# A decoder layer with a PEER expert sub-layer: 32 prompt tokens leave the dense expert pass for the gathered-row path (192 dense, 96 gathered)

## What is computed

```python
def _peer(h, wq, keys, u_tab, v_tab):          # per block of tokens tb
    q = (tb @ wq).reshape(TOK_BLOCK, PEER_HEADS, 2, PEER_DK)
    s = jnp.einsum('thpd,hpkd->thpk', q, keys)
    sv, si = lax.top_k(s, PEER_TOPK)
    ...                                         # top 16 of 16 x 16 sums, per head: fv, i1, i2
    eid = (i1 * PEER_NKEYS + i2).reshape(TOK_BLOCK, PEER_HEADS * PEER_TOPK)
    g = jax.nn.softmax(fv, axis=-1).reshape(TOK_BLOCK, PEER_HEADS * PEER_TOPK)
    hid = jax.nn.gelu(jnp.einsum('td,ted->te', tb, u_tab[eid]), approximate=False)
    return jnp.einsum('te,ted->td', (g * hid), v_tab[eid])
```

## Time and profile before

| | us |
|---|---|
| median of 3 runs | 2441.48 (2439.57 to 2441.72) |
| the profiled execution, its own time | 2438.12 |
| span of its profile | 2436.3 |
| gate rounds (line 1394 first to last) | 937.2 to 1026 |
| groups 0 and 1 | 1043.9 to 1172.0 |
| body(2), body(3) | 1172.0 to 1348.6 |
| body(4) to body(11) | 1348.6 to 2106.0 |
| body(12) | 2106.0 to 2193.5 |
| body(13), body(14) | 2193.5 to 2358.4 |
| V of the last group | 2358.4 to 2412.9 |

### The profile page before, as it was taken

The page is one execution under the profiler, slowest core; times in us unless marked ns, Lnnn a source line. Parts: engine busy times, 40 slices in busy tenths (PEclk is TensorE's granted clock), DMA queues, the critical chain, the costliest instruction groups (busy, mean ns, idle before and its releaser), DMA issues.

```text
span 2436.3 us, 38402 instructions
## 1 busy us (share of the span) xinstructions
PE 2257.6 (93%) x14756; PEld 1965.1 (81%) x14756; DVE 1645.2 (68%) x2907; ACT 925.3 (38%) x1034; POOL 355.9 (15%) x316
## 2 busy tenths in 40 slices
PE   7699999767979988999999999999999999999986
PEld 2298888436859988988999888888888888889985
DVE  1259777324345697866888777777877777766775
ACT  0332332342243314634444343343443443444432
POOL 1043000200000004510011212222212222010000
PEclk9899999778989999999999999999999999999999
DMA  9867776766634534576777999888989889877652
GB/s 382 349 234 288 286 277 226 279 242 225 236 127 145 163 131 153 216 250 234 266 273 282 344 345 324 327 338 323 345 307 345 334 319 341 290 275 266 209 176 91
DMA packets 152112, 643.36 MB, mean 264 GB/s; under 512 B 16721, under 2 KB 17105, under 8 KB 133649
## 3 DMA queue, kind: packets, MB, share of 16 engines
q1 hardware_dynamic: 122112, 444.65, 51.8%
q0 software_dynamic: 28400, 187.90, 19.9%
q10 hardware_dynamic: 1440, 8.56, 0.8%
HBM read 618.05 MB, written 22.99 MB: 263 GB/s over the span
## 4 chain that ended last, share of the span: by engine, by line
PE 83%; DVE 7%; DMA 6%; ACT 3%; issue 1%; POOL 0%; SPq 0%; DVEq 0%; ACTq 0%
PE vb L1429 17%; PE zb L1412 15%; PE vb L1431 7%; PE zb L1414 7%; PE zb L481 6%; PE zb L483 6%; PE zb L482 6%; DMA ada_first<-in_w_ada 3%; PE zb L1374 3%; PE vb L1452 3%; PE vb L1441 2%; PE vb L1394 2%; PE vb L1102 2%; DMA cache<-in_cv 1%; PE vb L1428 1%; DVE lo L465 1%
## 5 line engine op out<-in xcount | busy, mean ns | idle before, releaser
L456 ACT ACTIVATE hi<-raw 128x1024 fp32r<-128x1024 f32 x624 | 659.5, 1059 | 1046.9 <-PE vb L1429 374.6
L465 DVE TENSOR_TENSOR lo<-raw,hi 128x1024 fp32r<-128x1024 f32 x624 | 765.3, 1229 | 359.4 <-ACT hi L456 354.8
L1412 PE MATMUL zb<-act_hl,hi 128*128 128x448 f32 x1792 | 575.6, 376 | 3.0 <-DVE lo L465 3.0
L1429 PE MATMUL vb<-w_rest,hi 128*128 128x448 f32 x1536 | 521.2, 378 | 0.0
L1414 PE MATMUL zb<-act_hl,lo 128*128 128x224 f32 x1680 | 444.7, 265 | 0.0
L481 PE MATMUL zb<-act_hl,hi 128*128 128x288 f32 x1152 | 347.2, 301 | 37.2 <-DVE act_hl L1561 37.2
L1412 PEld LDWEIGHTS zb<-act_hl,hi 128*128 128x128 f32 x1792 | 334.5, 188 | 52.3 <-issue 24.3
L1431 PE MATMUL vb<-w_rest,lo 128*128 128x224 f32 x1280 | 342.9, 268 | 0.0
L482 PE MATMUL zb<-act_hl,hi 128*128 128x288 f32 x1152 | 341.9, 297 | 0.0
L483 PE MATMUL zb<-act_hl,lo 128*128 128x288 f32 x1152 | 341.3, 296 | 0.0
L1414 PEld LDWEIGHTS zb<-act_hl,lo 128*128 128x128 f32 x1680 | 321.0, 191 | 5.0
(11 more groups left out here) (266 smaller groups left out, 2438.1 us busy)
## 6 DMA issues: line engine op xcount, KB each, us to landing
raw<-in_v SPq DMA_DIRECT2D x256, 512.0 KB, 5.3
raw<-in_u SPq DMA_DIRECT2D x224, 512.0 KB, 5.5
raw<-in_w_in SPq DMA_DIRECT2D x80, 512.0 KB, 9.4
ada_first<-in_w_ada SPq DMA_DIRECT2D x64, 512.0 KB, 8.7
ada_mid<-in_w_ada SPq DMA_DIRECT2D x64, 512.0 KB, 5.3
ada_in<-in_w_ada SPq DMA_DIRECT2D x32, 512.0 KB, 9.0
raw<-in_w_out SPq DMA_DIRECT2D x32, 512.0 KB, 4.2
ada_last<-in_w_ada SPq DMA_DIRECT2D x32, 512.0 KB, 6.9
```

Source lines behind the costliest of these rows:

```text
L456: act.activation(hi[s][:, :], raw[s][:, :], ACT.Copy).then_inc(hi_ready, 1)
L465: dve.tensor_tensor(lo[s][:, :], raw[s][:, :], hi[s][:, :].bitcast(F32), ALU.subtract) \
L1412: last = pe.matmul(zb[:, bank, 0:2 * ND], w_h, act_hl[:, k, :, 0:ND], start=(k == 0), stop=(k == KC - 1))
L1429: last = pe.matmul(vb[:, bank, 0:2 * ND], v_h, w[:, e % 2, :, :], start=(e == 0), stop=(e == GI - 1))
```

## The change

ND goes from 224 to 192, so NGT is 96: 64 prompt tokens and the 32 samples. The gathered path begins in group 1's V part (unit -24) and its tokens end in body(14), the last but one group. Chunks now come every 12/13 of a unit to unit 329, in body(12); tokens every 3.9 units from unit 14 to unit 396, with 6 more units between each 32. The rows of the 64 prompt tokens fill the 128 partitions of `h_rows` (high part and remainder), so the samples' rows have a second set, `h_rows_s`, for which there are further turns, copies and subtractions while the queries are projected. The buffers are laid out anew for the smaller ND. `hid_4` becomes a ring of 64 columns. The sums of the values are now turned three times instead of two, and `residual_gathered`, which stood between body(13) and body(14) on DVE, is called from inside body(14). All loops over the dense tokens shrink: a pair has 576 columns instead of 672, and there are 24 gate rounds instead of 28. The core of the diff:

```diff
-ND = 224
+ND = 192
...
-ROWS = 2 * NGT
+NR = 64
+ROWS = 2 * NR
 def chunk_unit(c):
-    return 5 * c // 4
+    return 12 * c // 13 - 24
 def token_unit(t):
-    return (58 if t < TS else 64) + 19 * t // 4
+    return 14 + 39 * t // 10 + 6 * (t // TS)
...
-    h_rows = [at(f"h_rows{b}", [ROWS, 2, 512], F32R, (x_at + 14336, peer + 68096)[b]) for b in range(2)]
-    pick = at("pick", [ROWS, NGT], F32R, peer + 96768)
+    h_rows = at("h_rows", [ROWS, 3, 512], F32R, x_at + 12288)
+    h_rows3 = at("h_rows3", [ROWS, 512], F32R, peer + 68096)
+    h_rows_s = at("h_rows_s", [P, 2, 512], F32R, peer + 70144)
+    pick = at("pick", [ROWS, NR], F32R, peer + 96768)
+    pick_s = at("pick_s", [P, TS], F32R, peer + 97024)
...
-            for g in range(2, NG - 2):
-                pool.wait_ge(w_ready, PP * g + PP)
-                load_gates(g + 2)
+            for g in range(1, NG - 1):
+                if 2 <= g < NG - 2:
+                    pool.wait_ge(w_ready, PP * g + PP)
+                    load_gates(g + 2)
...
-                    for b2 in range(2):
-                        act.activation(h_rows[b2][:, :, :], vb[:, 2 * b2:2 * b2 + 2, :], ACT.Copy).then_inc(hs_copied, 1)
-                    for r in (0, NGT):
-                        last = act.activation(pick[r:r + NGT, :], ident[r:r + NGT, r:r + NGT], ACT.Copy)
+                    act.activation(h_rows[:, :, :], vb[:, 0:3, :], ACT.Copy).then_inc(hs_copied, 1)
+                    act.activation(h_rows3[:, :], vb[:, 3, :], ACT.Copy).then_inc(hs_copied, 1)
+                    for r in range(0, P, NR):
+                        act.activation(pick[r:r + NR, :], ident[r:r + NR, r:r + NR], ACT.Copy)
+                    for r in range(0, P, TS):
+                        last = act.activation(pick_s[r:r + TS, :], ident[r:r + TS, r:r + TS], ACT.Copy)
                     last.then_inc(hs_copied, 1)
+                if j in (3, 4):
+                    act.wait_ge(hs_turned, j - 1)
+                    act.activation(h_rows_s[:, j - 3, :], vb[:, 2, :], ACT.Copy).then_inc(hs_copied, 1)
...
-                for r in (0, NGT):
-                    last = pe.matmul(vb[r:r + NGT, k // 4, P * (k % 4):P * (k % 4) + P], hF[:, k, ND:T], ident,
+                for r in (0, NR):
+                    last = pe.matmul(vb[r:r + NR, k // 4, P * (k % 4):P * (k % 4) + P], hF[:, k, ND:SEQ], ident,
                                      start=True, stop=True)
             last.then_inc(hs_turned, 1)
+            def turn_samples(part):
+                pe.wait_ge(hs_split, 2 + 2 * part)
+                for k in range(4):
+                    for r in range(4):
+                        last = pe.matmul(vb[TS * r:TS * r + TS, 2, P * k:P * k + P],
+                                         hF[:, 8 * (r // 2) + 4 * part + k, SEQ:T], ident, start=True, stop=True)
+                last.then_inc(hs_turned, 1)
...
-                    pe.wait_ge(hs_copied, 3)
+                    pe.wait_ge(hs_split, 6)
                 else:
                     pe.wait_ge(dots_done, c)
                 t, j = c // 4, c % 4
-                pe.matmul(vb[:, 3, :], pick[:, t:t + 1].to_broadcast([ROWS, P]), h_rows[j // 2][:, j % 2, :],
-                          start=True, stop=True).then_inc(spread, 1)
+                if t < NR:
+                    row = h_rows[:, j, :] if j < 3 else h_rows3[:, :]
+                    one = pick[:, t:t + 1].to_broadcast([ROWS, P])
+                else:
+                    half = slice(NR * (j // 2), NR * (j // 2) + NR)
+                    row = h_rows_s[half, j % 2, :]
+                    one = pick_s[half, t - NR:t - NR + 1].to_broadcast([NR, P])
+                pe.matmul(vb[:, 3, :], one, row, start=True, stop=True).then_inc(spread, 1)
...
+                beside(c - 24)
+            u_quad(Q_PEER + 10, 2, 2, -8)
+            u_quad(Q_PEER + 11, 3, 3, -4)
...
+                if c >= 64 and c % 32 == 0:
+                    dve.wait_ge(hid_kept, c // 32 - 1)
...
+                if n == token_unit(NGT - 1) + 14:
+                    residual_gathered()
...
-                u_quad(Q_PEER + 8 + pp, 2, pp, 0, 16)
-            for g in range(2, NG - 2):
+                u_quad(Q_PEER + 8 + pp, 2, pp, 0, 16, 4 * pp - 16)
+            for g in range(2, NG - 1):
```

139 lines of the change are left out of this document (71 added, 68 removed).

## The result

The changed kernel takes 2506.8 us (median of 4 runs, 2499.8 to 2515.4) against 2440.5 of the kernel before on the same chip: a ratio of 1.027 with an interval of 1.025 to 1.030. The prediction was 2352 us, a gain. The measured time is 155 us above it, and the change has the other sign.

What follows compares the result with a forecast made beforehand. PE's columns were taken to bound the main loop. Stage terms sum to -89.8 us, from the profiled 2438.1 to 2348.3, and 3.4 more for the median gives 2352 us, range 2322 to 2402.

Steps and rivals of the forecast that it cites:

- PE's price of a pair: Dense products on PE: a pair falls from 0.315 to 0.270 us, giving back 173 us over 3840 pairs.
- Rival E's half form: Dense pairs on PE: only the narrow product stays unshrunk, pair 0.279 us, +35 us, 2387 us in all; chance 2%.
- A spread chunk costs 0.30: PE in the bodies: each spread chunk takes 0.30 us, four of them in a gathered token's 2.2 us.
- A full body has 34.7 chunks: Gathered bodies: 69.1 us of pairs, 10.4 of chunks and 7.8 of tokens make 87.3 us on PE.
- Rival C: Bodies: DVE becomes the bound through hand-offs, bodies of 93 us, +31, 2383 us in all; chance 10%.
- Rivals A and B: Gathered bodies: DMA queues bound at 371 GB/s (2398 us, 13%), or memory at 357 GB/s (2431 us, 3%).
- Rival D: Gathered bodies: u rows land too late, whole gain gone at 13.5 us mean landing, 2536 us at 15; chance 3%.
- Gate rounds, -12.3: Gate rounds before group 0: 28 become 24 (-7.1) and the 96 products beside them shrink by a seventh (-5.2).
- Group 0, -6: Group 0, 54.0 us: 160 narrower pairs would give -7.2, taken as -6 because a raw load shows.
- Group 1, -0.8: Group 1, 74.1 us: 224 narrower pairs -10.1, 31 added chunks +9.3; DVE tight, +3 at worst.
- Body(13), (14), -13.2: The two bodies before the last group: 164.9 to 151.7 us, with 11 tokens and an added turn of sums.
- The last group, -5: Last group, 54.5 us: 128 narrower pairs would give -5.8, but part is a chain through ACT and DVE.

Runs made afterwards that it cites:

- the third kernel: The changed kernel with the samples' spreads over all 128 partitions and one chunk per unit: 2414.0 us, 0.990 of the kernel before.
- the first experiment: The changed kernel with only the samples' spreads contracted over all 128 partitions, zero-filled, instead of 64: 2461.9 us, 1.010 of the kernel before.
- experiment 9: The kernel before with most dense pairs cut to 384 and 192 columns, sums of 32 dense tokens left incomplete: 2363.6 us, 0.970 of before.
- experiment 6: The kernel before with its 256 spreads on 128, 96, 64 or 32 partitions, changed every 26 spreads, some rows left out: 2502.6 us, single run.
- experiment 5: The changed kernel with full-height sample spreads, one chunk per unit, and v gathers fetching 16 rows, not 128, from the third token on: 2404.8 us, 0.986 of before.
- experiment 8: The kernel before with chunks coming two at a time every 2.5 units, so 128 units have two: 2640.8 us, single run.

## Why the prediction was wrong, point by point

The miss is 154.8 us. It closes: 62 from 2352 to the third kernel, 48 for the doubles (first to third experiment), 45 for the half-height spreads. In the other order the last two are 59 and 34; why they overlap by 11 us isn't shown.

- **PE's price of a pair** is the first step that failed. "Scaling the pair gives 0.315 x 576/672 = 0.270", measured 0.287. The check on 288-column products compared two products of 288 with one of 384 and one of 192. The experiments show both numbers to be right, 0.266 at (288, 288) and 0.284 to 0.287 at (384, 192): the total was the same, the split was not. Over 3840 pairs 0.017 would be 65 us, and the third kernel is 62 from the forecast. That the two agree so well is partly chance, as experiment 9 shows the price to hold only where PE has no gaps: from body(2) to body(12) the pairs are 48 us of the miss, while groups 0 and 1 and the end missed by more than their pairs. The other end of the price, 0.275 from pure column time, was no bound either.
- **Rival E's half form**, in which the narrow product gives nothing back, was the right mechanism. It had 2 in 100 and a pair of 0.279, still 0.008 short. The prediction shows no working for 0.279. With the forecast's own price per column, 64 columns less make 0.315 - 64 x 0.315/672 = 0.285, and with pure column time 0.315 - 64/2400 = 0.288; these put the time at 2410 and 2421, above the stated range and on either side of the third kernel's 2414. The point given for the whole rival, no gain from 0.2935 on, came out well: at 0.287 it leaves 3840 x 0.0065 = 25 us, and the third kernel gained 26.
- **"A spread chunk costs 0.30"** is the second step that failed. It holds for prompt tokens (0.61 around a spread, of which the pair's own part is 0.29 to 0.31). For the 128 sample chunks it was 0.65. The diff has it in plain sight, `slice(NR * (j // 2), ...)`, and no row of before shows a product of this height among full ones. It should have been bounded as an unknown operation. The Trainium skill's rule on a change of tiling mode (TensorEngine Tiling (Array Packing), "Key Properties"), told under experiment 6, would have opened a rival.
- **"A full body has 34.7 chunks"**, with nothing said about two of them in one unit, is the third, a wait put at nothing. The forecast priced 12/13 of a unit as a rate. What counted is that a second spread waits in PE's order for the dot of the first, with the whole dense stream queued behind it. I listed DVE's slack and never asked which engine waits for it. Before had one chunk at most per unit. The 30 doubles cost 48 us, 1.6 each.
- **Rival C**, DVE the bound, is not it: DVE is busy 77 to 79 us a body, as forecast (77.3; its narrower operations, 28 of 0.620 us less a seventh, are 2.5 and not 2.7), and the third kernel has the same DVE work in 92.0 us. PE did wait on DVE, but for one bank.
- **Rivals A and B**, DMA: refuted as a bound of 94.6 and 98.3. The queues moved 377 GB/s in body(4) of the changed kernel, above A's 371. Of them only the 9 us of experiment 5 were seen. **The friction of 2.2 us a body** was 1.1 in the third kernel.
- **Rival D** had the right side and the wrong reason: rows landed in 8.9 us in the median, never above 11.6, below its 13.5.
- **Gate rounds, -12.3**: first to last product now 931.6 to 1005.7 where it was 937.2 to 1024.9, 13.6 less. Right. All stages up to group 0 gave 20.1 in the changed kernel and 13.8 in the third; forecast 15.2.
- **Group 0, -6**: -1.8. **Group 1, -0.8**: +5.0, and +4.1 in the third kernel, beyond the +3 given as the worst. Experiment 9, with no chunks there, gained 2.1 where its pairs should have given 6, so these groups don't follow PE's columns. Part of it is the clock: one less the granted clock, times the length, comes to 9 us over the two groups of the third kernel (0.93 in both) and to 4 before (0.95 and 0.98). The rest stays open.
- **Body(13), (14), -13.2**: -0.9. 512 pairs at 0.017 are 9 of it. **The last group, -5**: +0.6. In its V part PE already waited six times, 8.3 us in all, for DVE's final sums before the change, and eleven times, 6.5 us, after it.
- **The range** of 2322 to 2402 reached to the rivals I had. All of them priced resources; none asked what an instruction of a new shape, or a second one in the same unit, does.

## What to carry to other kernels

Price a product by its own shape and by its neighbours': beside wide products the narrow one of a pair saved nothing here below some 230 columns, and one on 64 or 32 partitions between full ones cost 0.35 to 0.39 us more. Filling it with zeros to full height took that away at no price that these runs show. When an added step has a hand-off through a single buffer, look at where two of them fall together, not at their rate: the engine that issues in order stops with everything behind it, and behind most of its waits of 2 us and more it also went on at the lower clock here. A mean rate from one form of the work gives the mean rate of another only if the split inside stays the same.

## What the runs showed of the hardware that I had not expected

- In a stream of wide and narrow float32r products, each with its own weights, 96 to 224 narrow columns behind 448 wide ones change the mean pair by 0.008 us (0.306 to 0.314) and the median pair by 0.002. No pair of the table came under 0.22 us, 0.11 a product: (192, 192) takes 0.221 and (256, 128) 0.224.
- A spread on 96 partitions costs as much as one on 128 (0.654 against 0.645 us with its neighbours), on 64 or 32 it costs 0.39 us more, and it makes no difference which half is used.
- The queues ran at a share of 0.98 and 373 GB/s over 828 us, and a fifth less traffic gave back at most 0.7 us in 92.
- In the changed kernel, the first experiment's and that of experiment 8, every low stretch of the clock from body(2) to body(12) stands behind a wait of PE of 1.6 us or more. But not every such wait has one: 2.9 us at 1269 in the first experiment's kernel left the clock at 1.00, and the same length at 1266 in the changed kernel was followed by 4 us at 0.50.
